# Attention on one Trainium2 core: probabilities scaled before the transpose, heads in twin pairs with rotary row quarters, and a longer lag behind the scores

## The reference, cut to what matters

```python
# A: q, k, v of 8 heads, each 64 wide
sc = einsum('bihd,bjhd->bhij', q_blk, kb) * scale + bias[None]
p = softmax(where(valid, sc, NEG_INF)); o = einsum('bhij,bjhd->bihd', p, vb)
# B: 64 features normed per head, 32 rotated; the rotated key is shared by all heads
q_full = concatenate([q_nope, q_pe]);  k_full = concatenate([k_nope, broadcast(k_pe)])
sc = einsum('bqhd,bkhd->bhqk', q_blk, k_full) * scale
p = softmax(where(k_chunk <= q_chunk, sc, NEG_INF)); o = einsum('bhqk,bkhd->bqhd', p, v)
x = x + concatenate([out_a, out_b]) @ w_out
```

## Time and profile before

| | us |
|---|---|
| three runs | 1699.32, 1700.57, 1702.35 |
| median | 1700.57 |
| the profiled execution | 1701.04 |
| its span | 1699.2 |
| the attention on PE, from the first scores to the start of the last fraction of the output projection | 483.48 to 583.37 |

### The profile page before, as it was taken

How to read it: one execution, slowest core, us unless ns; L and a number is a source line. 1 busy time by engine, 2 the same in 40 slices (tenths; PEclk the granted TensorE clock), 3 DMA queues, 4 the chain that set the end, 5 groups by cost and what they waited for, 6 DMA issues and landing times.

```text
span 1699.2 us, 26804 instructions
## 1 busy us (share of the span) xinstructions
PE 1657.6 (98%) x10118; PEld 1355.5 (80%) x10118; DVE 946.7 (56%) x1389; ACT 433.2 (25%) x721; POOL 981.4 (58%) x596
## 2 busy tenths in 40 slices
PE   8999999999999999999999999998989999999998
PEld 6888888888767778888888867887868788888887
DVE  5666551226656346666562159987766766665103
ACT  4000000015866321111100031234353333233001
POOL 3666666766572377666677744611205576666774
PEclk9999999999999999999999989999999899999999
DMA  6444443333241134444443322210002232233332
GB/s 215 142 147 148 146 144 118 102 100 121 87 120 33 50 106 143 142 147 148 148 150 111 100 87 70 92 64 3 3 2 87 75 96 92 97 99 99 101 110 88
DMA packets 52112, 175.43 MB, mean 103 GB/s; under 512 B 6272, under 2 KB 8704, under 8 KB 51904
## 3 DMA queue, kind: packets, MB, share of 16 engines
q1 hardware_dynamic: 43056, 144.64, 26.3%
q10 hardware_dynamic: 8976, 29.63, 5.5%
HBM read 169.46 MB, written 2.10 MB: 101 GB/s over the span
## 4 chain that ended last, share of the span: by engine, by line
PE 93%; ACT 2%; DVE 2%; issue 1%; POOL 1%; DMA 0%; ACTq 0%; SPq 0%; DVEq 0%; POOLq 0%
PE banks L730 25%; PE banks L732 25%; PE banks L731 25%; PE banks L1199 4%; PE banks L1055 1%; PE banks L1028 1%; PE banks L762 1%; PE banks L1039 1%; PE banks L763 1%; PE banks L768 1%; PE banks L850 1%; PE banks L1025 1%; PE banks L1174 1%; PE banks L803 1%; PE banks L805 0%
## 5 line engine op out<-in xcount | busy, mean ns | idle before, releaser
L602 POOL TENSOR_TENSOR w_lo<-w_raw,w_hi 128x1024 fp32r<-128x1024 f32 x256 | 634.2, 2477 | 21.4
L600 POOL TENSOR_SCALAR w_hi<-w_raw 128x1024 fp32r<-128x1024 f32 x256 | 288.4, 1126 | 555.5 <-DMA w_raw<-in_slabs 477.0
L730 PE MATMUL banks<-h_hi,w_hi 128*128 128x512 f32 x1376 | 540.6, 393 | 0.6 <-POOL w_lo L602 0.6
L732 PE MATMUL banks<-h_hi,w_lo 128*128 128x512 f32 x1376 | 535.7, 389 | 0.0
L731 PE MATMUL banks<-h_lo,w_hi 128*128 128x512 f32 x1376 | 535.6, 389 | 0.0
L730 PEld LDWEIGHTS banks<-h_hi,w_hi 128*128 128x128 f32 x1376 | 258.4, 188 | 60.2 <-issue 5.8
L731 PEld LDWEIGHTS banks<-h_lo,w_hi 128*128 128x128 f32 x1376 | 258.4, 188 | 54.4 <-issue 1.7
L732 PEld LDWEIGHTS banks<-h_hi,w_lo 128*128 128x128 f32 x1376 | 258.3, 188 | 54.1
L730 PE MATMUL banks<-act_hi,w_hi 128*128 128x512 f32 (+1 forms) x550 | 209.7, 381 | 0.0
L731 PE MATMUL banks<-act_lo,w_hi 128*128 128x512 f32 (+1 forms) x550 | 209.3, 381 | 0.0
L732 PE MATMUL banks<-act_hi,w_lo 128*128 128x512 f32 (+1 forms) x550 | 209.3, 381 | 0.0
(11 more groups left out here) (389 smaller groups left out, 1840.8 us busy)
## 6 DMA issues: line engine op xcount, KB each, us to landing
w_raw<-in_slabs SPq DMA_DIRECT2D x260, 512.0 KB, 3.5
adaw<-in_ada ACTq DMA_DIRECT2D x48, 512.0 KB, 3.6
relb<-in_relb ACTq DMA_DIRECT2D x8, 256.0 KB, 2.9
out_y<-xT SPq DMA_DIRECT2D x16, 128.0 KB, 1.8
w_raw<-in_slabs SPq DMA_DIRECT2D x4, 256.0 KB, 5.2
xT<-in_x SPq DMA_DIRECT2D x1, 1024.0 KB, 8.3
block<-in_block ACTq DMA_DIRECT2D x1, 704.0 KB, 6.1
xT<-in_x SPq DMA_DIRECT2D x2, 256.0 KB, 3.8
```

The source lines that it names most:

```text
L600: nc.gpsimd.tensor_scalar(w_hi[:, r, :], w_raw[:, r, :], 1.0, 1.0, ALU.mult, ALU.mult).then_inc(S("w_hi"), 1)
L602: nc.gpsimd.tensor_tensor(w_lo[:, r, :], w_raw[:, r, :], w_hi[:, r, :], ALU.subtract).then_inc(S("w_split"), 1)
L730: mm(out, hi, rhs_hi, start=start, stop=False, skip_group_check=True)
L732: return mm(out, lo, rhs_hi, start=False, stop=stop, skip_group_check=True)
```

## The change

1. The probabilities are divided before they are transposed. GpSimd waits for `row_recip` and multiplies each head's exponentials in place by the reciprocal of their row sums (`probs_scaled`, 64 operations of 128xL); `turn` waits for that (`prob_scaled`) instead of for the exponentials. The widening, the spread, `keep_recips` and `out_scaled` are gone; `out_hi` and `out_lo` read the bank of the values, which alternates between 6 and 7 by pair.
2. In B the pairs come in twins: steps go through query block 1 of pair p, then of pair p+1, then block 2 of both, and so on. The scores of two steps are formed together: the 64 plain rows as in A, for one step and then the other, and then `rotary_scores`, four products of 32 rows, each on its own quarter of the partitions and into its own bank, added onto the first. The rotated keys are copied to the three other quarters by three DMAs (`key_rows_copied`); the 24 DMAs of `rows_moved` are gone. Only the rotary products report the scores of B.
3. turn and values lag one step more: PE at iteration i does turn(i-3) and values(i-4). In B, odd i has the scores of two steps and even i none. The pieces of the output projection lie at i = 31, 33 and 35.
4. In B `prob` has six slots instead of four (two in `relb`), and score_max(t) waits for turn(t-6) from t = 22 on. For t from 4 to 19 it still waits for turn(t-4).
5. On GpSimd the scaling of steps 0 and 1 stands ahead of the split of slab out1+2, and the nine rotary operations are spread over steps 4 to 14, one behind each scaling.
6. `out_lo` and `out_hi` of pair p come at iteration last_step(p)+5, on DVE behind score_max, keep_turned and row_recip, on ACT behind softmax.

```diff
--- before.py
+++ after.py
...
@@ -473,7 +472,11 @@
-    p, qb = divmod(t, NT)
+    if t < 4 * NT:
+        p, qb = divmod(t, NT)
+    else:
+        two, r = divmod(t - 4 * NT, 2 * NT)
+        p, qb = 4 + 2 * two + r % 2, r // 2
     return p, qb, P * (qb + 1)
@@ -485,14 +488,18 @@
+def prob_of(t, e):
+    n = 2 * (t % 4 if t < 4 * NT else (t - 4 * NT) % 6) + e
+    return (prob[:, n, :] if n < 8 else relb[:, n - 8, :])[:, 0:pair_step(t)[2]]
+def last_step(p):
+    return NT * p + NT - 1 if p < 4 else 4 * NT + 2 * NT * (p // 2 - 1) - 2 + p % 2
 def score_bank(t, e):
     return bank[4 + 2 * t + e if t < 2 else 2 * (t % 2) + e]
-def head_rows(m, p, e):
...
@@ -541,26 +548,17 @@
-    def rows_moved():
...
+    def key_rows_copied():
+        sp.wait_ge(S("roped"), 3)
+        for a in range(32, P, 32):
+            sp.dma_start(kr[a:a + 32, 0, :], kr[0:32, 0, :]).then_inc(S("key_rows"), 16)
     for n in range(in1 * RING, (out1 + 1) * RING):
         if n == SLAB_AT["out1"] + 3:
             rows_swapped()
         if n == SLAB_AT["out1"] + RING:
-            rows_moved()
+            key_rows_copied()
         sp.wait_ge(S("slab_done"), n + 1 - RING)
@@ -611,25 +609,26 @@
-    def recips_widened(t):
...
+    def probs_scaled(t):
         pool.wait_ge(S("row_recip"), t + 1)
-        out = rec_wide[p % 2][:, P * qb:P * qb + P].rearrange("p (e w) -> p e w", e=2)
-        nc.gpsimd.tensor_scalar(out, rec_of(t).unsqueeze(2).to_broadcast([P, 2, CH]), 1.0, None, ALU.mult)                    .then_inc(S("recips"), 1)
-    def rope_applied(k):
+        for e in range(2):
+            nc.gpsimd.tensor_scalar(prob_of(t, e), prob_of(t, e), rec_of(t)[:, e:e + 1], None, ALU.mult)\
+                .then_inc(S("prob_scaled"), 1)
+    def rope_applied(k, part):
         m, swapped = rotary[k]
-        if k == 0:
-            pool.wait_ge(S("rope_in"), 32 + 16 * 10)
         r = slice(0, m.shape[0])
-        nc.gpsimd.tensor_tensor(m, m, rope[r, 0, :], ALU.mult).then_inc(S("roped"), 1)
-        nc.gpsimd.tensor_tensor(swapped, swapped, rope[r, 1, :], ALU.mult).then_inc(S("roped"), 1)
-        pool.wait_ge(S("roped"), 3 * k + 2)
-        nc.gpsimd.tensor_tensor(m, m, swapped, ALU.add).then_inc(S("roped"), 1)
+        if part == 0:
+            if k == 0:
+                pool.wait_ge(S("rope_in"), 32 + 16 * 10)
+            nc.gpsimd.tensor_tensor(m, m, rope[r, 0, :], ALU.mult).then_inc(S("roped"), 1)
+        elif part == 1:
+            nc.gpsimd.tensor_tensor(swapped, swapped, rope[r, 1, :], ALU.mult).then_inc(S("roped"), 1)
+        else:
+            pool.wait_ge(S("roped"), 3 * k + 2)
+            nc.gpsimd.tensor_tensor(m, m, swapped, ALU.add).then_inc(S("roped"), 1)
@@ -673,23 +672,23 @@
             split(i * RING + r, r, i * 16 + 16)
-    for n in range(before * RING, SLAB_AT["out1"] + 3):
+    for n in range(before * RING, SLAB_AT["out1"] + 2):
         split(n, n % RING, 16 * (n // RING + 1))
-    pool.wait_ge(S("w_split"), SLAB_AT["out1"] + 3)
+    pool.wait_ge(S("w_split"), SLAB_AT["out1"] + 2)
     pool.wait_ge(S("hd_stat"), len(NORMED))
     for i, (a, b) in enumerate(((32, 64), (64, P))):
         nc.gpsimd.memset(g2b_t[a:b, :], 0.0).then_inc(S("masks_made"), 1)
         pool.wait_ge(S("masks_made"), 9 + i)
+    for t in range(2):
+        probs_scaled(t)
+    split(SLAB_AT["out1"] + 2, (SLAB_AT["out1"] + 2) % RING, 16 * ((SLAB_AT["out1"] + 2) // RING + 1))
     nc.gpsimd.memset(maskb[:, 0, :], 0.0).then_inc(S("masks_made"), 1)
     pool.wait_ge(S("masks_made"), 11)
     nc.gpsimd.memset(maskb[0:CH, 0, T - CH:T], -1e30).then_inc(S("masks_made"), 1)
-    rope_applied(0)
-    for t in range(8 * NT):
-        if t == NT:
-            rope_applied(1)
-            rope_applied(2)
-            pool.wait_ge(S("roped"), 9)
-        recips_widened(t)
+    for t in range(2, 8 * NT):
+        probs_scaled(t)
+        if NT <= t < 4 * NT and t % NT < 3:
+            rope_applied(t // NT - 1, t % NT)
     for n in range(SLAB_AT["out1"] + 3, (before + 2) * RING):
@@ -992,22 +991,9 @@
-    def recips_spread(p):
...
@@ -1015,28 +1001,36 @@
             pe.wait_ge(S("in1_raw"), len(MADE) + 4)
-        if t >= 4 * NT and qb == 0:
-            pe.wait_ge(S("rows_moved"), 96 * (p - 3))
         if t >= 2:
             pe.wait_ge(S("row_nmax"), 2 * (t - 1))
-        if p < 4:
-            for e in range(2):
-                e64 = slice(CH * e, CH * e + CH)
-                mm(out[e][:, 0:L], qa[e64, p, qs], ka[e64, p, 0:L], start=True, stop=True).then_inc(S("scores"), 1)
-            return
+        q, k = (qa, ka) if p < 4 else (qn, kn)
         for e in range(2):
-            mm(out[e][:, 0:L], head_rows(qn, p - 4, e)[:, qs], head_rows(kn, p - 4, e)[:, 0:L], start=True, stop=True)\
-                .then_inc(S("scores"), 1)
+            e64 = slice(CH * e, CH * e + CH)
+            last = mm(score_bank(t, e)[:, 0:L], q[e64, p % 4, qs], k[e64, p % 4, 0:L], start=True, stop=p < 4,
+                      skip_group_check=True)
+            if p < 4:
+                last.then_inc(S("scores"), 1)
+    def rotary_scores(t):
+        p, qb, L = pair_step(t)
+        if t == 4 * NT:
+            pe.wait_ge(S("key_rows"), 48)
+        pe.wait_ge(S("roped"), 6 if p < 6 else 9)
+        for i in range(4):
+            r = slice(32 * i, 32 * i + 32)
+            mm(score_bank(t + i // 2, i % 2)[:, 0:L], qr[r, (p - 4) // 2, P * qb:P * qb + P], kr[r, 0, 0:L],
+               start=False, stop=True, skip_group_check=True).then_inc(S("scores"), 1)
     def turn(t):
         _, qb, _ = pair_step(t)
         for e in range(2):
-            pe.wait_ge(S("probs"), 2 * t + e + 1)
+            pe.wait_ge(S("prob_scaled"), 2 * t + e + 1)
             if t >= 1:
                 pe.wait_ge(S(f"probT{e}"), t)
             for kt in range(qb + 1):
-                last = nc.tensor.transpose(bank[4 + e][:, P * kt:P * kt + P], prob[:, 2 * (t % 4) + e, P * kt:P * kt + P], ident)
+                last = nc.tensor.transpose(bank[4 + e][:, P * kt:P * kt + P], prob_of(t, e)[:, P * kt:P * kt + P], ident)
             last.then_inc(S(f"turned{e}"), 1)
@@ -1045,14 +1039,14 @@
             pe.wait_ge(S("row_nmax"), 4)
-        if qb == 0 and p >= 1:
-            pe.wait_ge(S("o_made"), 2 * p - 1)
+        if qb == 0 and p >= 2:
+            pe.wait_ge(S("o_made"), p - 1)
         for e in range(2):
             pe.wait_ge(S(f"probT{e}"), t + 1)
         for kt in range(qb + 1):
             for e in range(2):
                 h = 2 * (p % 4) + e
-                last = mm(bank[6][CH * e:CH * e + CH, P * qb:P * qb + P], v[:, kt, CH * h:CH * h + CH],
+                last = mm(bank[6 + p % 2][CH * e:CH * e + CH, P * qb:P * qb + P], v[:, kt, CH * h:CH * h + CH],
                           probT[t % 2][:, e, P * kt:P * kt + P], start=qb == 0 and kt == 0, stop=kt == qb,
@@ -1101,27 +1095,29 @@
         if m == 0:
-            pe.wait_ge(S("o_made"), 12)
+            pe.wait_ge(S("o_made"), 6)
         product(bank[m], at + m, (at + m) % RING, h_hi, h_lo, ks=range(6), stop=False)
-    for i in range(8 * NT + 3):
+    for i in range(8 * NT + 4):
         if i == 2:
             turn(1)
-        if 3 <= i + 1 < 8 * NT:
+        if 3 <= i + 1 < 4 * NT:
             scores(i + 1)
+        elif 4 * NT <= i + 1 < 8 * NT and (i + 1) % 2 == 0:
+            scores(i + 1)
+            scores(i + 2)
+            rotary_scores(i + 1)
         if i == 2:
             values(0)
-        if i >= 6 and i % NT == 2:
-            recips_spread((i - 6) // NT)
-        if 4 <= i < 8 * NT + 2:
-            turn(i - 2)
-        if i >= 4:
-            values(i - 3)
-        if 8 * NT - 1 <= i < 8 * NT + 2:
-            out1_begun(i - (8 * NT - 1))
+        if 5 <= i < 8 * NT + 3:
+            turn(i - 3)
+        if i >= 5:
+            values(i - 4)
+        if i in (8 * NT - 1, 8 * NT + 1, 8 * NT + 3):
+            out1_begun((i - 8 * NT + 1) // 2)
     for k in (6, 7):
-        pe.wait_ge(S("o_made"), 2 * k + 2)
+        pe.wait_ge(S("o_made"), k + 1)
         for m in range(3):
@@ -1679,12 +1675,11 @@
-        _, _, L = pair_step(t)
         if t >= 4:
             act.wait_ge(S("row_recip"), t - 3)
         for e in range(2):
             act.wait_ge(S("row_nmax"), 2 * t + e + 1)
-            p = prob[:, 2 * (t % 4) + e, 0:L]
+            p = prob_of(t, e)
             f(p, p, ACT.Exp, scale=-1.0, bias=of_step(row_nmax, t)[:, e:e + 1],
@@ -1697,24 +1692,16 @@
-    def keep_recips(p):
...
     def out_hi(p):
-        act.wait_ge(S("o_made"), 2 * p + 1)
-        f(h_hi[:, p, :], o_scaled, ACT.Copy).then_inc(S("o_kept"), 1)
-    for i in range(8 * NT + 4):
+        act.wait_ge(S("values"), last_step(p) + 1)
+        f(h_hi[:, p, :], bank[6 + p % 2], ACT.Copy).then_inc(S("o_kept"), 1)
+    for i in range(8 * NT + 5):
         if i in (2, 3):
             keep_turned(i - 2)
-        if 5 <= i < 8 * NT + 3:
-            keep_turned(i - 3)
+        if 6 <= i < 8 * NT + 4:
+            keep_turned(i - 4)
```

(72 more changed lines are left out.)

12 lines of the change are left out of this document (removed).

## The result

The changed kernel took 1710.46 us (median of 4 runs, 1709.43 to 1713.15), the kernel before 1700.43 (4 runs, 1699.32 to 1702.35): a ratio of 1.0061, 95% interval [1.0047, 1.0075]. That is 10 us slower; forecast were 1699.1 and a range up to 1706.0. The profiled execution took 1709.43, its span is 1707.6.

What follows compares the result with a forecast made beforehand. PE's own queue was taken to bound the attention stage: 6.0 us off its work, 4.4 back as waits, net -1.6, so 1699.4 against the profiled 1701.04. With the runs' median 0.47 lower, the forecast was 1699.1, range 1695.0 to 1706.0.

Steps and rivals of the forecast that it cites:

- I take the splits' price: GpSimd's scaling: 0.24 to 0.62 us for 1 to 4 blocks, 3.4 a pair, so PE would not wait for it.
- The rival: GpSimd sets the pace in A: scaling at 2.5 ns a column, 10.2 us a pair, 1705.2 in all; chance 17%.
- The spreads: PE's eight spreads of the reciprocals go, 0.435 us each, 3.5 us off PE's work.
- the second rival: B's 32-row rotary products don't run side by side: 1703.4 two at a time, 1712 one at a time; chance 7%.
- B's scores: PE in B: score products 1.35 us less a twin, turns 8 x 0.055 more; net 0.9 a twin, 1.8 for both.
- The two end waits: PE's waits behind the last scores, 0.28 us for `out_scaled` and 0.41 for `out_lo`, go: 0.7 off.
- scores(23) and scores(31): In B, PE waits 1.1 us at each for a maximum queued behind `out_lo` on DVE; 2.2 us in all.
- turn(19) and turn(27): In B, PE waits 0.5 us at each for DVE's copy of the previous turn, queued behind maxima; 1.0 in all.
- scores(19): From A to B, PE is 0.4 us late, since score_max(17) waits for turn(13), formed one iteration after scores(17).
- The one in A: At n = 4, score_max waits for a turn of the same iteration: 0.25 us in each of two pairs.
- The forecast of no change: Whole kernel: 1699.1 us, within 0.2% (3.4 us) of the kernel before; its own range 1697 to 1703, chance 58%.
- The third rival: DVE and ACT are always ahead, so PE has no new waits and the 6.0 us gain stands: 1694.6; chance 15%.

Runs made afterwards that it cites:

- the last experiment: The fastest kernel with one operator instead of two in GpSimd's scaling: 1705.77 us, ratio 1.0031 to the kernel before.
- the fastest kernel: The changed kernel with two operators in GpSimd's scaling, B's pairs one by one and the old lag of turn and values: 1694.59 us, ratio 0.9960 to the kernel before.

## Why the prediction was wrong, step by step

**The step that failed** is "I take the splits' price". The reason given, that the splits' rows are of the same class of instruction, was false in one operand that the code shows: a split is `1.0, 1.0, ALU.mult, ALU.mult` (L600), the scaling `..., None, ALU.mult`. The trace of before had one row of the latter form, the widening, at 0.53 us for 128 columns, and it lay within 0.07 of the truth (0.60); the splits' price was worked out as 0.24 there. The wait of PE for GpSimd, which "at that price it hides" put at nothing, came to 7.7 us. The row nearest in shape was not the row nearest in form. Two lengths would have told fixed cost from cost per column, and only one was in the trace, hence the wide bounds (9.6 to 14.3 us a pair); the measured 12.4 lies in them.

**The rival had the right bound, for a wrong reason, and the wrong size.** Its condition was an operator with a scalar from memory. That costs 0.07 us an instruction (689 against 616 ns with two operators); it is the missing second operator that makes the form dear. The 2.5 ns a column are right, but they were taken from two-source rows, and no run shows why the two agree. The rival also left out the 0.28 fixed for each of eight instructions: 10.2 instead of 12.4 us. It had 17%, and its time (1705.2) was 5 too low.

Where the 11.8 us between the changed kernel and the one with the second operator were lost can be read from the two timelines, counted from the first scores of each. At the start of the third A pair they are level (17.03 against 16.86 us). The two whole A pairs take 12.2 each against 9.0, so the first scores of B come 6.55 later, and the rotary products of the three-block step 11.8 later (57.54 against 45.73). From there on nothing more is lost. So two pairs paid for GpSimd's pace, not three, and 5.3 us fell on the way into B, where the rival had about 1: 2.1 are the last two waits for GpSimd (1.65 and 0.42), and most of the others are the clock.

**The clock added to it.** Before, the granted clock was 1.00 in all of this stage. After, in the stretch behind the 1.65 us wait:
```profile
532.60:539.40 6.80, 6.11 (x28) 3.76 (x28) 1.54 (x6) 1.80 (x5) 5.88 (x8) 0.51 0.01 2
```
Half clock is 1.2 GHz. With two operators the same work stood at 2.4 GHz:
```profile
526.10 0.88 PE L1049 MATMUL banks<-probT_even,va 128*64 128x128 f32 x12
526.90 1.56 PE L1009 MATMUL banks<-kn,qn 64*128 64x384 f32 x8
528.39 0.93 PE L1022 MATMUL banks<-kr,qr 32*128 32x384 f32 x8
```
From values to the quarters it is 2.29 us there and 4.26 (535.45 to 539.71) after, so the low clock cost 2.0. The turn ahead of them cost 0.5 more: 1.05 us (534.40 to 535.45) against 0.58 in the kernel with `out_lo` late, whose clock was still full there:
```profile
535.31 0.66 PE L1033 MATMUL banks<-both,prob 128*128 128x128 f32 x4 [0.89 <-POOL prob L616]
535.89 1.14 PE L1049 MATMUL banks<-probT_even,va 128*64 128x128 f32 x12
```
In this stage half clock stands only in the three kernels in which PE waits for GpSimd by 6.8 us or more (the change, `out_lo` late, and the old order with one operator). That the waits bring it is what these traces suggest; no run made PE idle that long by another means, and the size of a wait doesn't decide it. The two waits of 1.00 us for DVE in the kernel with the second operator alone left the clock at 1.00, and so did 2.8 us of waits in the changed kernel's pair from 499.20 to 511.38, where 3.1 us in the pair of the last experiment did not.

**PE's gains.** The spreads: right (8.97 less 8.53 is 0.44; I had 0.435). The quarters ran fully side by side: four products of 512 columns 1.07 us from start to start (545.89 to 546.96) against 1.06 forecast, and 3.0 for a twin, so the second rival fell. The Trainium skill's 3.07 for four row tiles ("TensorE: Matmul & The Clock Gate", Part 3), by which this would be an estimated 1.3 us, isn't borne out here. The plain rows took 1.06 and 1.49 for n = 2 and 3, as forecast, but some 0.35 more a twin in all, most of it at n = 4, where the wait of 1.0 us breaks the stream in two. Two single pairs take 20.2 us and a twin 19.8 of work, so B's scores gave 0.4 net a twin rather than 0.9. The two end waits went, as said.

**The waits.** Forecast and measured: scores(23) and scores(31) 1.1 and 1.00 each; turn(19) and turn(27) 0.5 and 0.47; scores(19) 0.4 and 0.29 (0.40 with two operators). The one in A was put at 0.25 in each of two pairs. With two operators it reads 0.28:
```profile
500.55 0.30 PE L1033 MATMUL banks<-both,prob 128*128 128x128 f32 x1 [0.28 <-DVE probT_odd L2196]
```
The A pair is longer by more than that, 9.00 us against 8.53, so the wait together with the break in the stream costs 0.47, nearly twice the forecast. With smaller gains and larger waits the stage moved by -0.2 us with two operators (forecast -1.6) and the time by nothing that can be measured. The forecast of no change would have stood at the splits' price, though 1.4 us of its gain were not there. The third rival, that the waits don't come, falls with the same rows.

**The move of `out_lo`.** The prediction's largest wait (2 x 1.1) is the one that a one-iteration delay removed, worth 2.5 of the stage. It had been read rightly as an order, not a load.

## What to carry to other kernels

Price an instruction by a row of the same form, operands and operators included, before one of the same shape; if only one length is in the trace, work the sum out with all of it as fixed cost and with all of it per column, and give the case in which an idle engine becomes the bound a chance to match. An engine that is busy for 58% of a span can have more work in one stage than the stage is long: add up its work there, and compare it with the period. Lagging a consumer by one more step isn't free where buffers are released by it: here it cost some 3 us. The scaling ahead of the transposes, which removed work from PE, was worth 4.1 us of the stage by itself and 6 by the medians (1694.59 against 1700.48).

## What was not expected of the hardware

- GpSimd's multiplication of a tile by a scalar from memory costs 0.28 us + 2.5 ns a column with one operator and 0.26 + 0.83 with two (371 ns for 128 columns, 688 for 512, in the fastest kernel). A constant in place of the scalar from memory takes off 0.07 us in either form (525 and 1486 ns with one operator, 297 and 616 with two). Asking for a product with 1.0 on top makes the instruction 2.3 times as fast for 512 columns; no run shows why. The Trainium skill ("GPSIMD Engine Reference", Engine selection) calls one-input operations roughly line-rate; that is borne out only for the form with two operators.
- TensorE's granted clock fell to half within a stage in three kernels, during or behind waits of 0.4 to 1.7 us that followed each other closely, and cost some 2.5 us on top of the waits in one of them. Outside this stage every kernel, the one before included, has stretches at half clock, and no run separates their share of the whole time.
